# Attention heads and a gated recurrence in eight shared steps: root spreads issued earlier on TensorE, one recurrence chunk per step in place of two

## What is computed

```python
rx, rgate, q, k, v, f_logit, ga, gb = jnp.split(rms_norm(x, mix_norm[i]) @ w_in[i], split_idx, axis=-1)

rx = causal_dwconv(rx, conv_w[i], conv_b[i])
# rg_lru: a = exp(log_a), u = sqrt(1 - a*a) * (i * rx);  h[t] = a[t] * h[t-1] + u[t] over the 256 tokens
ya = rg_lru(rx, ...)
ya = (ya * jax.nn.gelu(rgate)) @ w_rnn_out[i]

# per head (8 heads of 128): q and k are divided by their root mean square; s = q k^T + decay terms
# causal mask, softmax over the keys, product with v
yb = forgetting_attention(q, k, v, f_logit, ...) @ w_attn_out[i]

merged = jax.nn.sigmoid(ga + mb_a) * ya + jax.nn.sigmoid(gb + mb_b) * yb
x = x + merged @ w_o[i]
```

## Time and profile before

| what | value |
|---|---|
| runs, median (lowest to highest) | 3329.41 us (3328.5 to 3331.13), 3 runs |
| the profiled execution, its own time | 3330.55 us |
| its span | 3328.8 us |
| granted TensorE clock, mean over the span | 0.975 |
| TensorE / VectorE / ScalarE busy | 96% / 57% / 40% of the span |
| the head steps of layer 0 | about 376 to 470 us of the span |
| the head steps of layer 1 | about 1146 to 1235 us of the span |

### The profile page before, as it was taken

The page is one execution under the profiler, slowest core; times in us unless marked ns, Lnnn a source line. Parts: engine busy times, 40 slices in busy tenths (PEclk is TensorE's granted clock), DMA queues, the critical chain, the costliest instruction groups (busy, mean ns, idle before and its releaser), DMA issues.

```text
span 3328.8 us, 49855 instructions
## 1 busy us (share of the span) xinstructions
PE 3181.1 (96%) x21085; PEld 2799.8 (84%) x21085; DVE 1913.6 (57%) x2983; ACT 1346.4 (40%) x2046; POOL 2.3 (0%) x6
## 2 busy tenths in 40 slices
PE   7999899998999899998999999899999999999999
PEld 7999799998998889997888866578887888874898
DVE  5567656556557666556434379853335433455555
ACT  4445344445444444445322242432223222337544
POOL 0000000000000000000000000000000000000000
PEclk8999899999999999998999999999999999999999
DMA  6675437666665537657333343253334333242563
GB/s 194 181 209 159 159 126 213 185 195 199 188 201 173 180 102 208 187 166 220 102 102 89 89 127 101 88 140 89 102 92 124 114 89 101 89 140 76 165 184 108
DMA packets 671175, 478.86 MB, mean 144 GB/s; under 512 B 21487, under 2 KB 670057, under 8 KB 670953
## 3 DMA queue, kind: packets, MB, share of 16 engines
q1 hardware_dynamic: 670953, 475.68, 47.8%
HBM read 474.57 MB, written 1.05 MB: 143 GB/s over the span
## 4 chain that ended last, share of the span: by engine, by line
PE 80%; DVE 10%; ACT 4%; DVEq 3%; DMA 1%; issue 1%; SPq 0%; ACTq 0%
PE ps L560 24%; PE ps L562 24%; PE ps L561 24%; DVE Pp L1436 3%; DVE wl L1443 3%; DVEq L1895 2%; ACT wh L1048 2%; PE ps L634 1%; PE ps L999 1%; DMA raw<-in_ada_w 1%; DVEq L1486 1%; PE ps L976 1%; DVE Hl L1436 1%; PE ps L617 1%; ACT L1060 1%
## 5 line engine op out<-in xcount | busy, mean ns | idle before, releaser
L1443 DVE TENSOR_TENSOR wl<-raw,wh 128x1024 fp32r<-128x1024 f32 x780 | 951.2, 1224 | 920.2 <-ACT wh L1048 919.5
L1048 ACT ACTIVATE wh<-raw 128x1024 fp32r<-128x1024 f32 x780 | 816.5, 1057 | 1477.6 <-PE ps L562 1410.6
L560 PE MATMUL ps<-Hh,wh 128*128 128x256 f32 (+1 forms) x4048 | 1305.1, 322 | 44.4 <-DVE Hl L1436 13.8
L562 PE MATMUL ps<-Hh,wl 128*128 128x256 f32 (+1 forms) x4048 | 1287.3, 318 | 0.0
L561 PE MATMUL ps<-Hl,wh 128*128 128x256 f32 (+1 forms) x4048 | 1287.1, 318 | 0.0
L560 PEld LDWEIGHTS ps<-Hh,wh 128*128 128x128 f32 x4048 | 785.7, 194 | 111.0 <-issue 37.8
L561 PEld LDWEIGHTS ps<-Hl,wh 128*128 128x128 f32 x4048 | 786.1, 194 | 49.6 <-issue 2.4
L562 PEld LDWEIGHTS ps<-Hh,wl 128*128 128x128 f32 x4048 | 784.8, 194 | 48.2
L560 PE MATMUL ps<-Fh,wh 128*128 128x256 f32 (+1 forms) x1824 | 582.0, 319 | 13.2 <-DVE Fl L1805 7.7
L561 PE MATMUL ps<-Fl,wh 128*128 128x256 f32 (+1 forms) x1824 | 580.7, 318 | 0.0
L562 PE MATMUL ps<-Fh,wl 128*128 128x256 f32 (+1 forms) x1824 | 580.6, 318 | 0.0
(11 more groups left out here) (273 smaller groups left out, 1895.4 us busy)
## 6 DMA issues: line engine op xcount, KB each, us to landing
raw<-in_ffn_w_in SPq DMA_DIRECT2D x176, 512.0 KB, 5.2
raw<-in_ffn_wi SPq DMA_DIRECT2D x176, 512.0 KB, 5.2
raw<-in_ada_w SPq DMA_DIRECT2D x144, 512.0 KB, 4.5
raw<-in_w_in SPq DMA_DIRECT2D x112, 512.0 KB, 4.8
raw<-in_ffn_w_out SPq DMA_DIRECT2D x64, 512.0 KB, 4.3
raw<-in_ffn_wo SPq DMA_DIRECT2D x64, 512.0 KB, 4.3
raw<-in_ffn_w_out SPq DMA_DIRECT2D x32, 384.0 KB, 3.5
raw<-in_ffn_wo SPq DMA_DIRECT2D x32, 384.0 KB, 3.6
```

The lines of the kernel that those rows point to most:

```text
L560: nc.tensor.matmul(o, wh[:, u.par, kc, w], xh(kc), start=(kc == 0), stop=False)
L562: return nc.tensor.matmul(o, wl[:, u.par, kc, w], xh(kc), start=False, stop=(kc == kc_n - 1))
L1048: nc.scalar.activation(tile_of(wh[:, u.par], t), tile_of(raw[:, u.slot], t), ACT.Copy) \
L1443: V.tensor_tensor(tile_of(wl[:, u.par], t), tile_of(raw[:, u.slot], t), tile_of(wh[:, u.par], t).bitcast(F32), ALU.subtract).then_inc(lo_d ...
```

## The change

Two things. On TensorE, `spread(st + 1)` is issued at the end of step `st`, behind the second tile and ahead of `turn_probs(st - 1)` and `head_scores(st)`; only `spread(0)` stays between the two tiles. On VectorE and ScalarE the recurrence does one chunk in each of the eight steps, not two in each of the first four, and VectorE's low part of a chunk (`scanned_low`) moves one step later, ahead of the next step's first `lo`; the last one stands behind the loop. VectorE's program for the scaling of q and k is the same as before.

```diff
@@ TensorE
-                    spread(st)
+                    if st == 0:
+                        spread(0)
                     linear(u, part(Hh, T), part(Hl, T), T, tiles=(1,))
+                    if st + 1 < HEADS:
+                        spread(st + 1)
                     if st >= 1:
                         turn_probs(st - 1)
                     head_scores(st)
@@ ScalarE
                     head_exp(st)
-                    if st < 4:
-                        for j in (2 * st, 2 * st + 1):
-                            act.wait_ge(y_done, l * C + (j + 1))
-                            nc.scalar.activation(Fh[:, 0, j, :], Pp[:, j % 2, T:2 * T], ACT.Copy).then_inc(yh_done, 1)
+                    act.wait_ge(y_done, l * C + (st + 1))
+                    nc.scalar.activation(Fh[:, 0, st, :], Pp[:, st % 2, T:2 * T], ACT.Copy).then_inc(yh_done, 1)
@@ VectorE
+                def scanned_low(j):
+                    dve.wait_ge(yh_done, l * C + (j + 1))
+                    V.tensor_tensor(Fl[:, 0, j, :], Pp[:, j % 2, T:2 * T], Fh[:, 0, j, :].bitcast(F32), ALU.subtract) \
+                        .then_inc(ya_done, 1)
+
...
-                    two_chunks = (2 * st, 2 * st + 1)
-                    if st < 4:
-                        if st == 0:
-                            dve.wait_ge(root_done, l + 1)
-                        for j in two_chunks:
-                            stt(Xc[:, j, :], Xc[:, j, :], 0.5, keep[:, j, :], ALU.mult, ALU.mult)
+                    if st == 0:
+                        dve.wait_ge(root_done, l + 1)
+                    stt(Xc[:, st, :], Xc[:, st, :], 0.5, keep[:, st, :], ALU.mult, ALU.mult)
...
-                    if st < 4:
-                        for j in two_chunks:
-                            V.tensor_tensor_scan(Pp[:, j % 2, 0:T], decay[:, j, :], Xc[:, j, :], 0.0, ALU.mult, ALU.add)
-                        dve.drain()
-                        for j in two_chunks:
-                            V.tensor_tensor(Pp[:, j % 2, T:2 * T], Pp[:, j % 2, 0:T], Gb[:, j, :], ALU.mult) \
-                                .then_inc(y_done, 1)
-                        for j in two_chunks:
-                            dve.wait_ge(yh_done, l * C + (j + 1))
-                            V.tensor_tensor(Fl[:, 0, j, :], Pp[:, j % 2, T:2 * T], Fh[:, 0, j, :].bitcast(F32),
-                                            ALU.subtract).then_inc(ya_done, 1)
+                    V.tensor_tensor_scan(Pp[:, st % 2, 0:T], decay[:, st, :], Xc[:, st, :], 0.0, ALU.mult, ALU.add)
+                    dve.drain()
+                    V.tensor_tensor(Pp[:, st % 2, T:2 * T], Pp[:, st % 2, 0:T], Gb[:, st, :], ALU.mult) \
+                        .then_inc(y_done, 1)
+                    if st >= 1:
+                        scanned_low(st - 1)
+                scanned_low(HEADS - 1)
```

## The result

| what | before | with the change |
|---|---|---|
| median of five runs | 3329.75 us | 3356.26 us |
| lowest to highest | 3328.5 to 3338.45 us | 3352.57 to 3358.57 us |
| ratio, 95% interval | | 1.0067 [1.0056, 1.0078] |
| profiled execution, own time | 3330.55 us | 3358.57 us |
| its span | 3328.8 us | 3356.8 us |

The change makes the kernel slower: by 26.5 us between the medians, by 22 us (19 to 26) if the ratio is taken. The forecast was 3353.0 us, 23.6 above the median of before. The profiled execution is the slowest of its five, 2.3 us above their median.

What follows compares the result with a forecast made beforehand. TensorE, busy 96% of the span, was taken to bound the kernel. S4 to S7 +18.5, S0 to S4 -2.9, step 0 +1.5 and end of the stage +6.6 made +23.7 us: median 3353, whole range 3342 to 3367.

Steps and rivals of the forecast that it cites:

- S4 to S7: From head 4's softmax start on VectorE (S is that moment) to head 7's: 36.6 against 27.36 us a layer, +18.5 together.
- S0 to S4: From head 0's softmax start to head 4's: 48.8 and 48.7 us against 51.21 and 49.24, -2.9 together.
- step 0: First head step of each layer: two spreads ahead of its scores, 0.55 us, or 0.9 at layer 0's low clock; +1.5.
- end of the stage: Recurrent output projection waits for the last two low parts; L803 +3.3 us in each layer, +6.6 together.
- The turn: One softmax start to the next: TensorE can go after 9.00 us, then 0.55 + 0.33 + 1.95; 11.83, with clock 12.2.
- The spread: TensorE's four matmuls L783, 0.55 us: moved behind the wait for the unmoved scaling, they release nothing and lengthen the turn.
- The clock: Low TensorE clock behind waits, partly hidden, partly on the scores: 0.4 us more per turn, bounds 0 and 1.9.
- The rival in which every turn pays: Low clock costs 1.9 us in each of 14 turns, 26.6 on top of 17.7: 3374 us. Chance 0.15.
- The upper bound of 1.9: Most clock cost per turn, us: spread, turned probabilities and scores all at low level, 1.37 for scores, 0.5 for the others.
- The modulated turn: Second turn of each layer, holding the kept modulation, where TensorE idles and may slow: 12.8 us, between 11.8 and 13.9.
- The count of seven equal turns: Head steps of each layer: the long turn in every step, so the three from S4 to S7 all take 12.2 us.
- The wait on the low parts: First output tile of the recurrent projection waits 2 to 3 us in each layer; last parts ready at S7 + 5.5.

Runs made afterwards that it cites:

- The 32 fills: Changed kernel plus 32 result-less matmuls of 128 columns ahead of the moved spread, where TensorE would sit idle: 3367.57 us, ratio 1.0109.

## Why the prediction was right

The time was forecast at 3353.0 us and came out at 3356.26, within the forecast's own range of 3347 to 3362. By the terms of its sum, in the profiled executions:

| term | forecast | measured |
|---|---|---|
| S4 to S7, both layers | +18.5 | +9.63 + 8.47 = +18.1 |
| S0 to S4, both layers | -2.9 | -2.98 - 0.75 = -3.7 |
| step 0 | +1.5 | +0.67 + 2.18 = +2.9 |
| end of the stage | +6.6 | +3.79 + 3.38 = +7.2 |
| together | +23.7 | +24.4 |
| the rest of the program | 0 | +3.6 |

- **The turn.** Forecast 11.83 us without clock cost, measured 11.73 to 11.75 in six of the ten turns of steps 1 to 5: three at a clock of 1.00, three at 0.75 to 0.87 in which the slow tiles filled the wait. Each offset of the chain was met within 0.01 us, up to S + 9.00. That the turn is order and not busy time, on which the whole forecast stood, was shown in two ways: moving only the copy took it to 9.83, and moving only the scaling to 9.33.
- **The spread.** Forecast: it releases nothing as long as the scaling stays, and lies on the turn behind the wait. By itself it slows the kernel by 0.23%, and it gains only once the scaling follows it.
- **The clock.** Forecast 0.4 us in each turn, a mean. Measured it is 1.4 to 2.1 in four turns (13.33, 13.82, 13.59 and 13.15 against 11.74), 0.5 in the last turn of layer 0 (11.41 against 10.95) and 0 in the others: 7.4 us in fourteen turns, 0.5 per turn. The split that the forecast made, a part that hides in the turn and a part that falls on the work behind the wait, is the one that the trace shows; that the second part comes in full in a few turns was not foreseen. The rival in which every turn pays fails at its first step: a slow turn's tiles fill the next wait, so the idle of 2.68 us that it wants in every turn is there in five of fourteen. The upper bound of 1.9 was a slip: by its own ratio (3.21 to 1.84) the 0.88 us of spread and turned probabilities would grow by 0.66, not 0.5, and the bound would be 2.0, against 2.08 in the dearest turn.
- **The modulated turn.** Forecast 12.8, measured 11.75 and 11.74. L803 waits 2.1 us for the modulation in each layer, but the clock stays at 1.00 and the turn absorbs the wait, since TensorE would wait for the scaling anyway. This term was at the lower bound given; the dear turn came one step later.
- **The last turn.** The count of seven equal turns was wrong by one place: step 7 has no next head and so no spread, and the turn from S6 to S7 is 0.8 shorter (10.95). For the same reason the statement that L793 would leave the waits list was wrong: it still waits twice, 2.7 us. And L783 waits nine times, 18.0 us, not a dozen times at some 2.5.
- **Step 0 of layer 1.** Forecast +0.55, measured +2.18, from the stage's first tile to S0 12.41 us against 10.23. The timelines give the other 1.6. The rounding that the scaling stands behind begins 6.29 us after the first tile's start and not 5.24, since its weights landed later (in both profiles it waits for them), so TensorE is let go 1.05 later; and the scores, begun behind this wait, run in part at the low clock, 0.6 more. The prediction had named a late load as a thing it costed at nothing. Whether the late load comes from the change or from chance, no experiment shows.
- **The end.** L803 was forecast at S7 + 5.9 and came at S7 + 5.99 and S7 + 6.40. The wait on the low parts, forecast at 2 to 3 us in each layer, was 2.64 and 0.85.
- **Luck in the sum.** S0 to S7 of both layers came out 1.2 us below the 170.7 forecast because misses cancelled: the modulated turns 2.1 and the last turns 2.0 us shorter, four others together 1.8, against the long turns, 5.1 longer than 12.2 each.
- **Outside.** By the prediction's own words it is wrong if the time outside the two stretches changes by over 3 us, and 3.6 is over it. About 2 us of it lie between 788 and 992 us, in the feed-forward part ahead of the stage in layer 1, which the change does not touch; 2.3 us is what this execution is above its median. Nearly all of these 2 us is TensorE's clock: behind a wait of 1.8 us (0.7 before) the stretch from 818.18 to 823.93 has 0.70, where the same tile before had 1.00. Why the clock fell there in this execution stays open.

## What to carry to other kernels

On engines that work in order, write down the offsets of one step around the loop, S to S: that sum sets the period when it is longer than the bound engine's own work, however small the busy shares are, and it also forecasts edits well (10.95, 11.83, 9.9 and 9.35 against 10.94, 11.74, 9.83 and 9.33 measured, where the clock costs nothing). Put a wait behind the work that others need from this engine, not ahead of it: the copy that nobody needed for a step cost 1.9 us in nearly every turn. An operation issued early is worth nothing until its consumer is moved with it; spreading work evenly over all steps costs where it brings the long turn into steps that did not have it.

## What was not expected of the hardware

- **What a low clock costs depends on where it falls.** Of five turns in which TensorE idled for 2.44 to 2.46 us, four had the low level behind the wait (0.50 to 0.59 in the stretch that follows it) and one had 1.00, 2.74 us for the same work. There the low level cost 1.4 to 2.1 us. In the tiles of the next turn it cost nothing, down to a granted clock of 0.75 over the turn, because it only filled idle time. Where a turn has less slack it does cost: with the chunks alone (turns of 10.95), a turn at 0.77 was 11.77 us, TensorE busy throughout. A mean surcharge gave the right sum and the wrong turns.
- **A matmul of 128 columns is hardly cheaper than one of 256 here.** The 32 fills took 3.53 us from the first to the spread, 0.11 us each, at a clock of 1.00; the tiles' matmuls of 256 columns take 0.12 us each (24 in 2.88 us), and the three transposes of 128 columns took 0.33. By the instruction counts each comes with a weight load of its own. Halving the columns to fill or to shorten a wait brings almost nothing in this form.
